# Decode attention of the fox heads: one 128-column query block against one 32-column tile per head pair

## The chip, the cores and the metric

The kernel runs on one core of a Trainium2 chip. The metric is the device time of one execution in microseconds, the median of several runs. TensorE has two clock levels, 1.2 and 2.4 GHz; the profile gives the granted clock of a stretch as a share of the higher one (PEclk). In the profile PE is TensorE's matrix passes, PEld its weight loads, DVE VectorE, ACT ScalarE, POOL GpSimd and SP SyncE, which issues the DMAs.

## What is computed

One layer of a hybrid encoder: a feed-forward block, a token mixer with two groups of attention heads (latent attention, "MLA", and forgetting attention, "fox"), and a second feed-forward block. There are 1,024 prompt frames, and 8 running streams of 16 new frames, each with 512 cached rows. The change touches only the fox heads of the 8 streams. Cut to that:

```python
# per stream: q (16, 8, 64), k and v (512 + 16, 8, 64), cumulative log forgets lq, lk
s = einsum('qhd,khd->hqk', q, k) * 64 ** -0.5
s = s + (lq - lk)                      # per head
s = where(k_pos <= q_pos, s, -inf)
p = softmax(s, axis=-1)
o = einsum('hqk,khd->qhd', p, v)
```

## The kernel before

The program is written in stages, one block of engine programs each: feed-forward 1, input projection, latents, MLA of the prompt, `sample_setup`, `sample_attention` (the 8 streams), fox of the prompt, output projection, feed-forward 2. The feed-forward blocks are some three quarters of the time and are left as they are.

`sample_attention` runs the 8 streams in a loop of two (b = 0 and 1), with the last two written out. The order on each engine is the order of the code; engines meet at semaphores. In one step PE does, for stream n and the one after it:

1. `stream`: transposes of the probabilities of stream n (L1514 cached, L1518 new rows), into PSUM; ACT copies them to `pT` and `pTn`.
2. `transpose_keys`: transposes of the keys of stream n + 1 (L1480), in seven groups over two PSUM banks, which ACT and DVE empty in turn (L1385, L1380). Names: `ckv` and `kr` are the MLA keys, `fk` the fox keys.
3. `score` of stream n + 1 (L1485, L1502): `scores` has 128 partitions, 16 for each of the 8 heads, and a column for each of the 528 keys. The MLA scores come from `qc` and `qr`. The fox scores come from `qf`, the block-diagonal query: its 512 depth rows (8 heads of 64) lie in 4 chunks `c` of 128, and chunk c has the 128 query columns with all but those of heads 2c and 2c + 1 at zero. So 4 matmuls accumulate over c, each 128 rows deep and 128 columns wide, over 512 cached keys (`fkT`) and again over 16 new ones (`knT`); one more matmul (`qa` with `aug_r`) adds the forget sums, and one the mask.
4. The value products of stream n (L1531 over 4 row groups `r` of the cache, L1532 for the new rows): `out_bank[0]` for MLA with `ckv`, then `out_bank[1]`, which is `o_ps`, for fox. The fox product takes all 128 probability columns with all 512 value columns (8 heads of 64), so 128 x 512 results, of which each partition needs its own head's 64.

All these matmuls are f32; the trace shows each of them as two passes with a weight load each, the transposes as one. DVE takes the row maxima (L1428, L1432), then `outputs`: the reciprocal of the sums, the MLA result (L1440), and for fox three steps: `picked` = `o_ps` times a 0/1 head mask, 128 x 512 (L1444), `folded` = the sum over the 8 heads (L1446), and that times the reciprocal into `o_fox` (L1448). ACT takes the exponents of stream n + 1 (L1396) while PE does step 4. POOL copies the queries of the next stream into `qc`, `qr`, `qf`, `qa` (L1369 to L1372). After the last stream all engines meet, and the stage `back` (L1564 on) turns the results.

```python
for m in range(2):
    pe.wait_ge(pt_ok, n2 + 2)
    ...
    rows, new_rows, w = (ckv[b], cn[b], KVL) if m == 0 else (fv[b], vn[b], FW)
    for r in range(CK):
        pe.matmul(out_bank[m][:, 0:w], pT[m][:, r, :], rows[:, r, :], start=(r == 0), stop=False)
```

Of the kernel before, what the change touches and what calls it, by code (L numbers as in the profile page):

```python
# [8 lines left out]
P = 128  # L9
D = 1024  # L10
KD = D // P
SEQ, DECB, DECT, PAST = 1024, 8, 16, 512
# [464 lines left out]
H = 8  # L477
# [649 lines left out]
KEYS = PAST + NEW  # L1127
BH = DECB * H
# [23 lines left out]
def sample_setup(nc, ident, q_sample, select, rows_in, load_first_keys, s):  # L1152
# [3 lines left out]
    with Tools(nc, "setup") as k:  # L1156
# [12 lines left out]
        with k.block() as block:  # L1169
# [59 lines left out]
            def _(dve):  # L1229
# [6 lines left out]
                for j in range(2):  # L1236
                    for c in range(4):
                        src = flip[64 * j:64 * j + 64, 1, c * P:c * P + P].rearrange("p (b t) -> p b t", t=NEW)
                        last = dve.tensor_scalar(s["qbd"][64 * j:64 * j + 64, c, :, (2 * c + j) * NEW:(2 * c + j + 1) * NEW], src, 64 ** -0.5, None, ALU.mult)
# [36 lines left out]
def sample_attention(nc, ident, ident_bf, mask_bf, head_pick, s, cache_ckv, cache_krope, cache_fk, cache_fv, fox_rows, ckv_out, o_rows, prompt_rows, prompt_loaded, keys_in):  # L1276
# [4 lines left out]
    with Tools(nc, "dec") as k:  # L1281
# [16 lines left out]
        picked = k.sb("picked", [P, H, 64])  # L1298
# [26 lines left out]
        inverse_ok, picked_ok, folded_ok, mla_taken, fox_taken = [k.sem(n) for n in ("inverse_ok", "picked_ok", "folded_ok", "mla_taken", "fox_taken")]  # L1325
        LOADS, STAGES, FLIPS = 3, 4, 7
# [12 lines left out]
        with k.block() as block:  # L1339
# [84 lines left out]
            def _(dve):  # L1424
# [9 lines left out]
                def outputs(i, b):  # L1434
                    n, n2 = i * 2 + b, i * 4 + 2 * b
                    dve.wait_ge(exp_ok, n2 + 2)
                    dve.reciprocal(inverse[:, b, :], total[:, b, :]).then_inc(inverse_ok, 1)
                    dve.wait_ge(inverse_ok, n + 1)
                    dve.wait_ge(pv_ok, n2 + (4 + 1))
                    dve.tensor_scalar(o_mla[:, bass.ds(n, 1), :], out_bank[0][:, 0:KVL].unsqueeze(1), inverse[:, b, 0:1], None, ALU.mult).then_inc(mla_taken, 1)  # L1440

                    dve.wait_ge(pv_ok, n2 + (4 + 2))
                    dve.wait_ge(folded_ok, n + 1)
                    dve.tensor_tensor(picked[:, :, :], o_ps[:, :].rearrange("p (h d) -> p h d", h=H), head_pick.unsqueeze(2).broadcast_to([P, H, 64]), ALU.mult).then_inc(fox_taken, 1)  # L1444
                    dve.wait_ge(fox_taken, n + 2)
                    dve.tensor_reduce(folded[:, :], picked[:, :, :].rearrange("p h d -> p d h"), axis=AX.X, op=ALU.add).then_inc(picked_ok, 1)  # L1446
                    dve.wait_ge(picked_ok, n + 1)
                    dve.tensor_scalar(o_fox[:, bass.ds(n, 1), :], folded[:, :].unsqueeze(1), inverse[:, b, 1:2], None, ALU.mult).then_inc(folded_ok, 1)  # L1448
# [16 lines left out]
            def _(pe):  # L1465
# [4 lines left out]
                for free in (mla_taken, fox_taken, folded_ok):  # L1470
                    pe.sem_inc(free, 1)
# [16 lines left out]
                def score(i2, b, last_stream=None):  # L1488
                    n = i2 * 2 + b
                    new = bass.ds(n * NEW, NEW)  # L1490
                    def copied(groups):

                        for e in range(2):
                            pe.wait_ge(flip_ok[e], i2 * FLIPS + (flip_number(b, groups) + 1 - e) // 2)

                    pe.wait_ge(staged, n * STAGES + STAGES)
                    copied(KC + 1)
                    product(cached_part[0], [(qc[b][:, c, :], ckvT[:, c, :]) for c in range(KC)] + [(qr[b][:, :], krT[:, :])], False)
                    if last_stream is not None:
# [5 lines left out]
                    product(cached_part[1], [(qf[b][:, c, :], fkT[:, c, :]) for c in range(4)] + [(qa[b][:, :], s["aug_r"][:, 0:PAST].rearrange("q (p r) -> q r p", r=CK))], False).then_inc(s_ready, 1)  # L1505

                def stream(i, b, follows):
# [17 lines left out]
                    for m in range(2):  # L1525
                        pe.wait_ge(pt_ok, n2 + 2)
                        if m == 1:
                            pe.wait_ge(fox_taken, n + 1)
                        rows, new_rows, w = (ckv[b], cn[b], KVL) if m == 0 else (fv[b], vn[b], FW)
                        for r in range(CK):  # L1530
                            pe.matmul(out_bank[m][:, 0:w], pT[m][:, r, :], rows[:, r, :], start=(r == 0), stop=False)  # L1531
                        pe.matmul(out_bank[m][:, 0:w], pTn[m][:, :], new_rows[:, :], start=False, stop=True).then_inc(pv_ok, 1)  # L1532
# [183 lines left out]
def layer(nc, x_prompt, x_sample, cache_ckv, cache_krope, cache_fk, cache_fv, cache_logf, g1_pre, g1_post, w1_gu, w1_down,  # L1716
# [11 lines left out]
    with Tools(nc, "all") as k:  # L1728
# [3 lines left out]
        tri, ones, head_pick = k.sb("tri", [P, P]), k.sb("ones", [P, P]), k.sb("head_pick", [P, H])  # L1732
        consts_in = k.sem("consts_in")

        with Tools(nc, "consts") as c:
            wide = c.sb("wide", [P, 2 * P + NEW])
            with c.block() as block:
# [8 lines left out]
                def _(dve):  # L1746
# [3 lines left out]
                    dve.tensor_copy(mask_bf[:, :], wide[:, :])  # L1750

# [34 lines left out]
        with Tools(nc, "mix") as m:  # L1786
            fox_loaded = m.sem("fox_loaded")
            logf, krope = m.sb("logf", [P, TT, H]), m.sb("krope", [P, TT, ROPE])
            with Tools(nc, "lat") as l:
# [15 lines left out]
                    qbd=[P, 4, DECB, P], qcT=[P, KC, DECB, H, NEW], aug_l=[P, DECB, P], knT=[P, 4, P], cnT=[P, KC, P], krnT=[ROPE, P],  # L1805
# [13 lines left out]
            with Tools(nc, "dec_all") as d:  # L1819
# [10 lines left out]
                sample_attention(nc, ident, ident_bf, mask_bf[:, 2 * P:2 * P + NEW], head_pick[:, :], own, cache_ckv, cache_krope, cache_fk, cache_fv, fox_rows, ckv_out, acc, fox_prompt_rows, fox_loaded, keys_in)  # L1830
# [55 lines left out]
```

## Time and profile before

| | |
|---|---|
| median of 3 runs | 2846.46 us (2845.43 to 2851.75) |
| span of the profiled execution, which is all the time that its page gives | 2846.8 us |
| PE busy | 2649.1 us, 93% |
| weight loads / DVE / ACT / POOL busy | 82% / 33% / 23% / 15% |
| mean granted clock of TensorE | 0.958 |
| the 8 streams of `sample_attention` | 1433 to 1639 us |

Busy shares are means over the whole span, and weight loads run beside passes. What the streams cost is read from a timeline of PE between 1433 and 1639 us, where a row gives the start, the time to the end of the last pass in it, engine, line, operation, tiles and shape, how many passes, and in brackets how long PE was idle before it and who ended that. Passes are pipelined, so that the time a row really takes is the distance from its start to the start of the next row.

### The profile page before, as it was taken

What the parts mean: (1) busy time and instruction counts of PE and PEld (TensorE: products, weight loads), DVE (VectorE), ACT (ScalarE), POOL (GpSimd) and SP (SyncE); (2) the same over time, 40 slices, a digit from 0 to 9 for tenths busy, and PEclk for the clock granted to TensorE, in tenths of its full rate; (3) what the DMA queues carried; (4) which work ended last, traced back from release to release, by engine and by line L of the source; (5) the groups of instructions that cost most, each with busy time, mean ns of one, the idle gap of its engine ahead of it and who ended that gap; (6) DMA issues with size and microseconds to landing.
All of it is one profiled execution on the core that took longest, in us unless ns stands there. A gap on an engine that the chain in (4) does not pass through costs nothing. (4 is left out here: it accounts for less than half of the span.)

```text
span 2846.8 us, 35924 instructions
## 1 busy us (share of the span) xinstructions
PE 2649.1 (93%) x14251; PEld 2340.2 (82%) x14251; DVE 938.1 (33%) x1612; ACT 658.4 (23%) x1138; POOL 437.9 (15%) x229
## 2 busy tenths in 40 slices
PE   5999999999996997889889969989899999999997
PEld 5999999999995887768745448867899999999996
DVE  4222222222226222554422254434222222222224
ACT  4111111111124011434222214433311111111112
POOL 1111111111113000000000001022111111111112
PEclk8999999999998998989989979989899999999999
DMA  4111111111014221100133030022211111111103
GB/s 152 45 44 44 44 44 44 44 44 44 15 63 156 78 80 39 38 9 0 54 116 115 31 119 0 0 94 92 81 45 44 44 44 44 36 38 44 44 15 141
DMA packets 134646, 161.61 MB, mean 57 GB/s; under 512 B 9648, under 2 KB 105008, under 8 KB 132528
## 3 DMA queue, kind: packets, MB, share of 16 engines
q1 hardware_dynamic: 134576, 160.66, 17.5%
q8 instruction: 47, 0.77, 0.1%
q14 instruction: 23, 0.19, 0.0%
HBM read 138.04 MB, written 22.60 MB: 56 GB/s over the span
## 5 line engine op out<-in xcount | busy, mean ns | idle before, releaser
L65 PE MATMUL ffn_gate_ps<-all_xT_hi,ffn_gu_hi 128*128 128x384 f32 x1056 | 355.8, 337 | 20.4 <-DVE all_xT_lo L163 12.2
L378 DVE TENSOR_TENSOR ffn_prod<-ffn_up_ps,ffn_silu 128x384 f32<-128x384 f32 x132 | 73.6, 558 | 893.2 <-ACT ffn_silu L346 893.2
L66 PE MATMUL ffn_gate_ps<-all_xT_lo,ffn_gu_hi 128*128 128x384 f32 x1056 | 354.9, 336 | 0.0
L67 PE MATMUL ffn_gate_ps<-all_xT_hi,ffn_gu_lo 128*128 128x384 f32 x1056 | 354.9, 336 | 0.0
L65 PE MATMUL ffn_up_ps<-all_xT_hi,ffn_gu_hi 128*128 128x384 f32 x1056 | 352.9, 334 | 0.0
L67 PE MATMUL ffn_up_ps<-all_xT_hi,ffn_gu_lo 128*128 128x384 f32 x1056 | 352.7, 334 | 0.0
L66 PE MATMUL ffn_up_ps<-all_xT_lo,ffn_gu_hi 128*128 128x384 f32 x1056 | 352.7, 334 | 0.0
L346 ACT ACTIVATE ffn_silu<-ffn_gate_ps 128x384 f32<-128x384 f32 x132 | 64.9, 492 | 1222.3 <-PE ffn_up_ps L67 1222.3
L65 PE MATMUL ffn_down_ps<-ffn_dn_hi,ffn_a_hi 128*128 128x512 f32 x792 | 309.2, 390 | 2.2 <-DVE all_acc L391 2.1
L391 DVE TENSOR_TENSOR all_acc<-ffn_down_ps,all_acc 128x512 f32<-128x512 f32 x360 | 246.0, 690 | 195.1 <-PE ffn_down_ps L67 195.1
L67 PE MATMUL ffn_down_ps<-ffn_dn_hi,ffn_a_lo 128*128 128x512 f32 x792 | 308.6, 390 | 0.0
L66 PE MATMUL ffn_down_ps<-ffn_dn_lo,ffn_a_hi 128*128 128x512 f32 x792 | 308.6, 390 | 0.0
L315 POOL TENSOR_TENSOR ffn_gu_lo<-gu_raw,ffn_gu_hi 128x2048 fp32r<-128x2048 f32 x43 | 197.5, 4613 | 460.1 <-ACT ffn_gu_hi L339 460.1
L319 POOL TENSOR_TENSOR ffn_dn_lo<-ffn_dn_raw,ffn_dn_hi 128x2048 fp32r<-128x2048 f32 x22 | 101.4, 4607 | 855.1 <-ACT ffn_dn_hi L352 855.1
L65 PEld LDWEIGHTS ffn_gate_ps<-all_xT_hi,ffn_gu_hi 128*128 128x128 f32 x1056 | 200.0, 189 | 22.4 <-DVE all_xT_lo L163 12.8
L66 PEld LDWEIGHTS ffn_gate_ps<-all_xT_lo,ffn_gu_hi 128*128 128x128 f32 x1056 | 200.1, 189 | 0.8
L67 PEld LDWEIGHTS ffn_gate_ps<-all_xT_hi,ffn_gu_lo 128*128 128x128 f32 x1056 | 199.8, 189 | 0.0
L65 PEld LDWEIGHTS ffn_up_ps<-all_xT_hi,ffn_gu_hi 128*128 128x128 f32 x1056 | 198.2, 188 | 0.0
L66 PEld LDWEIGHTS ffn_up_ps<-all_xT_lo,ffn_gu_hi 128*128 128x128 f32 x1056 | 198.2, 188 | 0.0
L67 PEld LDWEIGHTS ffn_up_ps<-all_xT_hi,ffn_gu_lo 128*128 128x128 f32 x1056 | 198.2, 188 | 0.0
L65 PEld LDWEIGHTS ffn_down_ps<-ffn_dn_hi,ffn_a_hi 128*128 128x128 f32 x792 | 148.7, 188 | 34.9 <-DVE all_acc L391 4.7
L67 PEld LDWEIGHTS ffn_down_ps<-ffn_dn_hi,ffn_a_lo 128*128 128x128 f32 x792 | 148.7, 188 | 31.1
(348 smaller groups left out, 3947.7 us busy)
## 6 DMA issues: line engine op xcount, KB each, us to landing
gu_raw<-in_w_ffn_gu SPq DMA_DIRECT2D x88, 512.0 KB, 5.1
ffn_dn_raw<-in_w_ffn_down SPq DMA_DIRECT2D x22, 1024.0 KB, 4.9
h<-all_acc SPq DMA_DIRECT2D x18, 512.0 KB, 2.9
dec_high_fk<-in_cache_fox_k SPq DMA_DIRECT2D x8, 1024.0 KB, 5.3
dec_x_fv<-in_cache_fox_v SPq DMA_DIRECT2D x8, 1024.0 KB, 4.7
out_fox<-inp_stage SPq DMA_DIRECT2D x27, 256.0 KB, 2.0
in_raw<-in_w_in SPq DMA_DIRECT2D x6, 1024.0 KB, 7.5
fox_x_rows<-out_fox SPq DMA_DIRECT2D x3, 2048.0 KB, 14.8
```

Source lines behind the costliest of these rows:

```text
L65: pe.matmul(out, w_hi, x_hi, start=first, stop=False)
L66: pe.matmul(out, w_hi, x_lo, start=False, stop=False)
L67: return pe.matmul(out, w_lo, x_hi, start=False, stop=last)
L315: pool.tensor_tensor(gu_lo[j][:, :, :], gu_raw[j][:, :, :], plain(gu_hi[j][:, :, :]), ALU.subtract).then_inc(lo_ok, 1)
L319: pool.tensor_tensor(dn_lo[:, :, :], dn_raw[:, :, :], plain(dn_hi[:, :, :]), ALU.subtract).then_inc(lo_ok, 1)
L346: act.activation(silu[:, u % 2, :], gate_ps[:, u % 2, 0:GN], ACT.Silu).then_inc(silu_ok, 1)
L378: dve.tensor_tensor(prod[:, u % 2, :], up_ps[:, u % 2, 0:GN], silu[:, u % 2, :], ALU.mult).then_inc(prod_ok, 1)
L391: dve.tensor_tensor(dst, down_ps[:, m % DR, :], dst, ALU.add).then_inc(added, 1)
```

## The change

The fox query of a stream becomes 4 tiles of 32 columns (`PAIR`: two heads of 16 frames), one for each chunk c; a tile's result goes to its own 32 partitions, at 0, 32, 64 and 96, and no chunk is added to another. `head_pairs` does so for the cached and for the new keys; forget sums and mask are added over all 128 partitions as before. In the value product each pair's 32 probability columns meet only that pair's 128 value columns: 4 matmuls of 32 x 128 for each row group in the place of one of 128 x 512, and 4 for the new rows. On DVE `pair_pick` (which of the two heads a partition belongs to) times the reciprocal gives two scales for each partition, and two operations of 128 x 64 make `o_fox`. POOL copies a quarter as much for `qf`, and the new keys into `kf_new` besides.

```diff
+PAIR = 2 * NEW
...
-        qf = [k.sb(f"qf{b}", [P, 4, P]) for b in range(2)]
+        qf = [k.sb(f"qf{b}", [P, 4, 2 * NEW]) for b in range(2)]
+        kf_new = [k.sb(f"kf_new{b}", [P, 4, NEW]) for b in range(2)]
...
-        LOADS, STAGES, FLIPS = 3, 4, 7
+        LOADS, STAGES, FLIPS = 3, 5, 7
...
+                        pool.tensor_copy(kf_new[b][:, :, :], s["knT"][:, :, bass.ds(n * NEW, NEW)]).then_inc(staged, 1)
...
+                    dve.tensor_scalar(head_scale[:, b, :], pair_pick, inverse[:, b, 1:2], None, ALU.mult).then_inc(scaled_ok, 1)
+                    dve.wait_ge(scaled_ok, n + 1)
                     dve.wait_ge(pv_ok, n2 + (4 + 2))
-                    dve.wait_ge(folded_ok, n + 1)
-                    dve.tensor_tensor(picked[:, :, :], o_ps[:, :].rearrange("p (h d) -> p h d", h=H), head_pick.unsqueeze(2).broadcast_to([P, H, 64]), ALU.mult).then_inc(fox_taken, 1)
...
-                    dve.tensor_reduce(folded[:, :], picked[:, :, :].rearrange("p h d -> p d h"), axis=AX.X, op=ALU.add).then_inc(picked_ok, 1)
...
-                    dve.tensor_scalar(o_fox[:, bass.ds(n, 1), :], folded[:, :].unsqueeze(1), inverse[:, b, 1:2], None, ALU.mult).then_inc(folded_ok, 1)
+                    dve.tensor_scalar(folded[:, :], o_ps[:, 0:64], head_scale[:, b, 0:1], None, ALU.mult).then_inc(half_ok, 1)
+                    dve.wait_ge(half_ok, n + 1)
+                    dve.scalar_tensor_tensor(o_fox[:, bass.ds(n, 1), :], o_ps[:, 64:P].unsqueeze(1), head_scale[:, b, 1:2], folded[:, :].unsqueeze(1), ALU.mult, ALU.add).then_inc(fox_taken, 1)
...
+                    def head_pairs(out, keys):
+
+                        for c in range(4):
+                            pe.matmul(out[c * PAIR:c * PAIR + PAIR, :], qf[b][:, c, :], keys(c), start=True, stop=False)
+
...
-                    product(new_part[1], [(qf[b][:, c, :], s["knT"][:, c, new]) for c in range(4)] + [(qa[b][:, :], s["aug_r"][:, PAST:KEYS])], True)
+                    head_pairs(new_part[1], lambda c: kf_new[b][:, c, :])
+                    pe.matmul(new_part[1], qa[b][:, :], s["aug_r"][:, PAST:KEYS], start=False, stop=False)
...
+                    head_pairs(cached_part[1], lambda c: fkT[:, c, :])
...
+                    pe.wait_ge(fox_taken, n + 1)
+                    for r in range(CK):
+                        for c in range(4):
+                            rows = slice(c * PAIR, c * PAIR + PAIR)
+                            pe.matmul(o_ps[rows, 0:P], pT[1][:, r, rows], fv[b][:, r, c * P:c * P + P], start=(r == 0), stop=False)
+                    for c in range(4):
+                        rows = slice(c * PAIR, c * PAIR + PAIR)
+                        last = pe.matmul(o_ps[rows, 0:P], pTn[1][:, rows], vn[b][:, c * P:c * P + P], start=False, stop=True)
+                    last.then_inc(pv_ok, 1)
```

On PE, from the fox scores over the cached keys to the value products of one step, before (a row ends in the partitions and columns of the result, and in how many such matmuls follow each other):

```order
L1485 MATMUL dec_scores<-dec_fkT,dec_qf 128x512 x4
L1485 MATMUL dec_scores<-dec_x_aug_r,dec_qa 128x512
L1524 REGISTER_ALU
L1531 MATMUL dec_pT_ps<-dec_ckv,dec_pT 128x256 x4
L1532 MATMUL dec_pT_ps<-dec_cn,dec_pTn 128x256
L1531 MATMUL dec_o_ps<-dec_x_fv_4734,dec_pT 128x512 x4
L1532 MATMUL dec_o_ps<-dec_vn,dec_pTn 128x512
```

and changed:

```order
L1501 MATMUL dec_scores<-dec_fkT,dec_qf 32x512 x4
L1514 MATMUL dec_scores<-dec_x_aug_r,dec_qa 128x512
L1533 REGISTER_ALU
L1536 MATMUL dec_pT_ps<-dec_ckv,dec_pT 128x256 x4
L1537 MATMUL dec_pT_ps<-dec_cn,dec_pTn 128x256
L1542 MATMUL dec_o_ps<-dec_x_fv_4735,dec_pT 32x128 x16
L1545 MATMUL dec_o_ps<-dec_vn,dec_pTn 32x128 x4
```

Nothing changes place: the four score matmuls keep their 512 columns and become 32 partitions each, and five fox value matmuls of 512 columns become twenty of 128.

On DVE, the outputs of one step, before:

```order
L1437 RECIPROCAL dec_inverse<-dec_total 128x2
L1440 TENSOR_SCALAR dec_o_mla<-dec_pT_ps,dec_inverse 128x256
L1444 TENSOR_TENSOR dec_picked<-dec_o_ps,all_head_pick 128x512
L1446 TENSOR_REDUCE dec_folded<-dec_picked 128x64
L1448 TENSOR_SCALAR dec_o_fox<-dec_folded,dec_inverse 128x64
```

and changed:

```order
L1440 RECIPROCAL dec_inverse<-dec_total 128x2
L1443 TENSOR_SCALAR dec_o_mla<-dec_pT_ps,dec_inverse 128x256
L1445 TENSOR_SCALAR dec_head_scale<-all_pair_pick,dec_inverse 128x2
L1448 TENSOR_SCALAR dec_folded<-dec_o_ps,dec_head_scale 128x64
L1450 SCALAR_TENSOR_TENSOR dec_o_fox<-dec_o_ps,dec_head_scale,dec_folded 128x64
```

The scale stands ahead of the wait for the fox product; behind that wait two small operations follow in the place of three, two of which read 512 columns.

## Rows read from the trace of the kernel before

**Rows 1.** Page, its head and part 1: busy us (share) and instructions of each engine.

```profile
span 2846.8 us, 35924 instructions
...
PE 2649.1 (93%) x14251; PEld 2340.2 (82%) x14251; DVE 938.1 (33%) x1612; ACT 658.4 (23%) x1138; POOL 437.9 (15%) x229
```

**Rows 2.** Windows, two steps: length, busy us (instructions) of PE, PEld, DVE, ACT, POOL, clock.

```profile
1493.80:1517.80 24.00, 22.16 (x93) 12.25 (x92) 6.89 (x12) 5.68 (x12) 1.42 (x4) 1.00 0.33 114
1517.80:1544.30 26.50, 25.53 (x93) 13.69 (x92) 6.13 (x11) 6.17 (x13) 1.42 (x4) 0.87 0.30 103
```

**Rows 3.** Timeline of PE, one step.

```profile
1496.24 3.70 PE L1531 MATMUL dec_o_ps<-dec_x_fv,dec_pT 128*128 128x512 f32 x8
1499.87 1.12 PE L1532 MATMUL dec_o_ps<-dec_vn,dec_pTn 16*128 16x512 f32 x2
1500.92 1.09 PE L1514 MATMUL dec_pT_ps<-all_ident,dec_p_sb 128*128 128x128 f32 x8
...
1502.07 1.04 PE L1480 MATMUL dec_flip<-all_ident,dec_high_ckv_in 128*128 128x128 f32 x8
1504.26 0.61 PE L1480 MATMUL dec_flip<-all_ident,dec_high_kr 128*32 128x128 f32 x4 [1.15 <-DVE dec_ckvT L1380]
1504.71 0.60 PE L1480 MATMUL dec_flip<-all_ident,dec_high_fk 128*128 128x128 f32 x4
...
1510.44 1.07 PE L1485 MATMUL dec_scores<-dec_x_knT,dec_qf 128*128 x8
1511.36 0.38 PE L1485 MATMUL dec_scores<-dec_x_aug_r,dec_qa 128*128 128x16 f32 x2
...
1512.45 3.70 PE L1485 MATMUL dec_scores<-dec_fkT,dec_qf 128*128 128x512 f32 x8
1515.99 1.96 PE L1485 MATMUL dec_scores<-dec_x_aug_r,dec_qa 128*128 128x512 f32 x2
1517.77 1.91 PE L1531 MATMUL dec_pT_ps<-dec_ckv,dec_pT 128*128 128x256 f32 x8
```

**Rows 4.** Timeline of PE: the same score passes in five other steps.

```profile
1442.99 5.34 PE L1485 MATMUL dec_scores<-dec_fkT,dec_qf 128*128 128x512 f32 x8
...
1463.69 5.23 PE L1485 MATMUL dec_scores<-dec_fkT,dec_qf 128*128 128x512 f32 x8
...
1536.11 6.56 PE L1485 MATMUL dec_scores<-dec_fkT,dec_qf 128*128 128x512 f32 x8
...
1563.31 6.62 PE L1485 MATMUL dec_scores<-dec_fkT,dec_qf 128*128 128x512 f32 x8
...
1589.46 5.40 PE L1485 MATMUL dec_scores<-dec_fkT,dec_qf 128*128 128x512 f32 x8
```

**Rows 5.** Timeline of DVE in the step of rows 3: the fox outputs.

```profile
1501.03 0.69 DVE L1444 TENSOR_TENSOR dec_picked<-dec_o_ps,all_head_pick 128x512 f32<-128x512 f32 x1 [4.01 <-PE dec_o_ps L1532]
1501.76 1.07 DVE L1446 TENSOR_REDUCE dec_folded<-dec_picked 128x64 f32<-128x512 f32 x1
1502.97 0.25 DVE L1448 TENSOR_SCALAR dec_o_fox<-dec_folded,dec_inverse 128x64 f32 x1 [0.15 <-DVE dec_folded L1446]
1503.52 0.69 DVE L1380 COPY dec_ckvT<-dec_flip 128x512 f32<-128x512 f32 x1 [0.29 <-issue]
```

**Rows 6.** Timeline of ACT in that step: the second of the two exponents.

```profile
1495.43 0.69 ACT L1396 ACTIVATE dec_p_sb<-dec_scores,dec_nmax 128x528 f32<-128x528 f32 x1
```

**Rows 7.** Timeline of all engines at the end of the last stream.

```profile
1636.95 0.69 DVE L1444 TENSOR_TENSOR dec_picked<-dec_o_ps,all_head_pick 128x512 f32<-128x512 f32 x1 [4.12 <-PE dec_o_ps L1532]
...
1638.72 0.25 DVE L1448 TENSOR_SCALAR dec_o_fox<-dec_folded,dec_inverse 128x64 f32<-128x64 f32 x1
...
1639.30 0.41 PE L1564 MATMUL dec_flip<-all_ident,dec_o_mla 128*128 128x128 f32 x2 [2.39 <-PEq L1339]
```

**Rows 8.** Line L1480, the narrow weight loads: ns min/median/max, first and last start, form.

```profile
L1480 PEld LDWEIGHTS dec_flip<-all_ident,dec_high_kr x32: 93/97/150, 1434.5 to 1606.8; 128*32 128x32 f32 x32
```

More of the change, by code:

```diff
@@ L1238, in _ @@
                         src = flip[64 * j:64 * j + 64, 1, c * P:c * P + P].rearrange("p (b t) -> p b t", t=NEW)
-                        last = dve.tensor_scalar(s["qbd"][64 * j:64 * j + 64, c, :, (2 * c + j) * NEW:(2 * c + j + 1) * NEW], src, 64 ** -0.5, None, ALU.mult)
+                        last = dve.tensor_scalar(s["qbd"][64 * j:64 * j + 64, c, :, j * NEW:(j + 1) * NEW], src, 64 ** -0.5, None, ALU.mult)
                 last.then_inc(moved, 1)
@@ L1273, in _, with sample_attention @@
                 dve.tensor_tensor(grid, grid, s["l_new"][BH:P, :].unsqueeze(1).broadcast_to([BH, BH, NEW]), ALU.mult)
[L1276 removed]
+def sample_attention(nc, ident, ident_bf, mask_bf, pair_pick, s, cache_ckv, cache_krope, cache_fk, cache_fv, fox_rows, ckv_out, o_rows, prompt_rows, prompt_loaded, keys_in):
     with Tools(nc, "dec") as k:
@@ L1469, in _ @@
                 pe.sem_inc(pv_ok, 4)
-                for free in (mla_taken, fox_taken, folded_ok):
+                for free in (mla_taken, fox_taken):
                     pe.sem_inc(free, 1)
@@ L1504, in score @@
                     copied(FLIPS)
-                    product(cached_part[1], [(qf[b][:, c, :], fkT[:, c, :]) for c in range(4)] + [(qa[b][:, :], s["aug_r"][:, 0:PAST].rearrange("q (p r) -> q r p", r=CK))], False).then_inc(s_ready, 1)
+                    head_pairs(cached_part[1], lambda c: fkT[:, c, :])
+                    pe.matmul(cached_part[1], qa[b][:, :], s["aug_r"][:, 0:PAST].rearrange("q (p r) -> q r p", r=CK), start=False, stop=True).then_inc(s_ready, 1)
                 def stream(i, b, follows):
@@ L1524, in stream @@
                     pe.wait_ge(kept, i * 2 + (b + 3))
[L1525 to L1532, printed above, removed]
+                    pe.wait_ge(pt_ok, n2 + 2)
+                    for r in range(CK):
+                        pe.matmul(out_bank[0][:, 0:KVL], pT[0][:, r, :], ckv[b][:, r, :], start=(r == 0), stop=False)
+                    pe.matmul(out_bank[0][:, 0:KVL], pTn[0][:, :], cn[b][:, :], start=False, stop=True).then_inc(pv_ok, 1)
+                    pe.wait_ge(fox_taken, n + 1)
+                    for r in range(CK):
+                        for c in range(4):
[5 more added lines that the diff above has]
+                    last.then_inc(pv_ok, 1)
                 transpose_keys(0, 0)
@@ L1731, in layer @@
         mask_bf = k.sb("mask_bf", [P, 2 * P + NEW], BF16)
-        tri, ones, head_pick = k.sb("tri", [P, P]), k.sb("ones", [P, P]), k.sb("head_pick", [P, H])
+        tri, ones, head_pick, pair_pick = k.sb("tri", [P, P]), k.sb("ones", [P, P]), k.sb("head_pick", [P, H]), k.sb("pair_pick", [P, 2])
         consts_in = k.sem("consts_in")
@@ L1750, in _ @@
                     dve.tensor_copy(mask_bf[:, :], wide[:, :])
+                    dve.tensor_reduce(pair_pick[:, :], head_pick[:, :].rearrange("p (c j) -> p j c", j=2), axis=AX.X, op=ALU.add)
         acc = k.sb("acc", [P, TT, D])
@@ L1804, in layer @@
                 (Region(nc, "dec_x", xT_at, (PT * D + TT * H * QW) * 4), dict(
-                    qbd=[P, 4, DECB, P], qcT=[P, KC, DECB, H, NEW], aug_l=[P, DECB, P], knT=[P, 4, P], cnT=[P, KC, P], krnT=[ROPE, P],
+                    qbd=[P, 4, DECB, 2 * NEW], qcT=[P, KC, DECB, H, NEW], aug_l=[P, DECB, P], knT=[P, 4, P], cnT=[P, KC, P], krnT=[ROPE, P],
                     qrT=[ROPE, DECB, H, NEW], aug_r=[P, KEYS], l_new=[P, NEW], fv0=[P, CK, FW], fv1=[P, CK, FW])))
@@ L1829, in layer @@
                 sample_setup(nc, ident, q_sample, select, setup_in, load_first_keys, own)
-                sample_attention(nc, ident, ident_bf, mask_bf[:, 2 * P:2 * P + NEW], head_pick[:, :], own, cache_ckv, cache_krope, cache_fk, cache_fv, fox_rows, ckv_out, acc, fox_prompt_rows, fox_loaded, keys_in)
+                sample_attention(nc, ident, ident_bf, mask_bf[:, 2 * P:2 * P + NEW], pair_pick[:, :], own, cache_ckv, cache_krope, cache_fk, cache_fv, fox_rows, ckv_out, acc, fox_prompt_rows, fox_loaded, keys_in)
             fox_prompt(nc, ident, ident_bf, mask_bf[:, P:2 * P], tri[:, :], ones[:, :], logf, fox_prompt_rows, fox_loaded, acc,
```

6 lines of the change are left out of this document (2 added, 4 removed).

## The prediction

> **What bounds the kernel now.** I read the page first: PE is busy for 2649.1 of 2846.8 us [rows 1], so the question is what a PE instruction costs in the stage that is changed. Then the windows of that stage, cut at the steps of the stream loop: in 24.00 us PE is busy for 22.16, and DVE, ACT and POOL for 6.89, 5.68 and 1.42 [rows 2]. PE bounds each step. Its weight loads (12.25 us) run beside its passes: the two add up to more than the window. The timeline of PE then gives the prices as distances from start to start [rows 3]: the fox scores over the cached keys take 1515.99 - 1512.45 = 3.54 us for 8 passes (0.4425 each), those over the new keys 1511.36 - 1510.44 = 0.92 (0.115 each), and the whole fox value product 1500.92 - 1496.24 = 4.68. So 9.14 us of a 24 us step are what the change rewrites. In five of the eight steps the cached scores take longer [rows 4]; the window of the third of these has a mean granted clock of 0.87 against 1.00 [rows 2], so a part of it ran at 1.2 GHz. Against the 3.70 of [rows 3] the five cost 1.64 + 1.53 + 2.86 + 2.92 + 1.70 = 10.65 us. Off PE, DVE's fox outputs run from 1501.03 to 1503.22, and its next copy starts at 1503.52 [rows 5]; PE waits 1.15 us for that copy [rows 3]. ACT's exponents end at 1496.12 [rows 6], 4.8 us before PE asks for them at 1500.92.
>
> **The change, part by part.** The profiled execution spans 2846.8 us; the median of the runs is 2846.46. I sum differences and take them from the median.
>
> *Fox scores.* The number of passes and their columns stay: 4 matmuls, two passes each. A pass over 512 columns takes its time whether 128 or 32 query columns are loaded, so a gain needs passes of different tiles to run side by side. No row shows two tiles at once, so the price is bounded: above by passes one after the other (3.54 and 0.92 us, no gain), below by all four tiles at once (two passes: 0.885 and 0.23 us). I take a value between. In the program's order the two passes of a tile follow each other, and the second must wait for the first, since both stream through the same 32 columns of the array. If passes start in order, what can overlap is the second pass of one tile and the first of the next: 4 matmuls take 5 pass times and not 8 or 2. That is 5 x 0.4425 = 2.21 us (-1.33) and 5 x 0.115 = 0.575 (-0.345).
>
> *Fox value product.* It becomes 20 matmuls, 40 passes, of 128 columns with 32-column weights. A pass of just this shape is in the trace, the turn of the rotary keys (128 rows, 32 columns loaded, 128 streamed): 4 in 1504.71 - 1504.26 = 0.45 us, 0.1125 each [rows 3]. One after the other that is 4.50 us, all four tiles at once 1.13, and with the overlap of neighbours 21 x 0.1125 = 2.36. The new rows are only 16 deep: their two passes cost 1.05 us now against 2 x 3.63/8 = 0.91 for full ones [rows 3], so a group of such passes adds 0.14, which I keep. 2.50 in the place of 4.68: -2.18.
>
> *Going in and out of tiles.* The narrow turns stand among full passes and lose nothing (0.1125 against 0.115 for the score passes of the new keys); the 16-deep pair loses 0.14. The three tiled groups are 128 deep and 32 wide like the narrow turns, so I take 0 for two of them; at 0.14 it would be 0.28 us more in each of 8 steps, 2.2 us in all.
>
> Together -3.855 us a step, and 8 steps: **-30.8**. The exponents still hide: after the scores 2.4 us of MLA products remain ahead of the fox product (1493.80, the window's start, to 1496.24 [rows 2, 3]), and ACT is done 2.3 us after the scores.
>
> *DVE.* Behind the fox product 0.69 + 1.07 + 0.15 + 0.25 us [rows 5] become two operations of 128 x 64 with a wait between, 0.25 + 0.15 + 0.25. DVE is free 1.5 us earlier. In steps where DVE empties the first bank of keys (three show this wait; [rows 3] has the first) its copy can then start when the first four turns are done, near 1502.6 and not at 1503.52; what is late next is PE's own turns. I count 0.85 us three times: **-2.5**. After the last stream PE waits for DVE to end [rows 7]: 2.02 us from 1636.95 become 0.65: **-1.35**.
>
> *The rest at nothing.* POOL copies a quarter of `qf` and adds `kf_new`; it works 1.42 us in a step of 24 [rows 2]. The fill of `qbd` gets smaller. `pair_pick` is one small DVE operation at the program's start: +0.25 at most, by the smallest row of [rows 5]; I count it. The arrays behind `pair_pick` move by 32 bytes; no row prices that. The clock I leave as it is; the 10.65 us of [rows 4] could vanish, or recur in other steps at up to 2.92 each (8 x 2.92 - 10.65 = +12.7).
>
> Sum: -30.8 - 2.5 - 1.35 + 0.25 = -34.4, so 2846.46 - 34.4 = **2812**.
>
> **The rivals.**
>
> *A. All four tiles run at once.* The second pass of a tile does not hold up the next tile. Scores 0.885 and 0.23, values 10 x 0.1125 + 0.14 = 1.27: -6.76 a step, -54.1 in 8, with the other terms -57.7: **2789**. For it: the tiles share neither columns nor result partitions. Against: each tile has two passes in a row. The Trainium skill ("TensorEngine Tiling (Array Packing)", Theoretical Speedup) gives up to 4x for a dimension of 32; no run here shows it so far, and by it the time would be that of this rival.
>
> *B. Nothing overlaps, loads stay hidden.* The tiles then are the same passes in other shapes: values 4.64 for 4.68, scores unchanged. Only DVE's terms remain: -0.3 - 3.6 = -3.9, **2842.5** (2845 with the price of going in and out). For it: every pair of passes in the trace is strictly one behind the other. Under 0.2% (5.7 us), which is about what a measurement of this kernel tells from no change.
>
> *C. Nothing overlaps and the loads show: slower.* A pass now uses one tile's columns, and the load for the next tile waits until it is over. A narrow load takes 0.097 us [rows 8], and there are 40 in the value product for 10. 48 loads (40 and the 8 of the cached scores) x 0.097 = 4.66 us a step, 37.3 in 8, less 3.9: **2880**. It decides from 3.9/(8 x 48) = 10 ns of each load in the open. Against: today's loads are hidden, though all of them use the full depth of 128 rows like the passes that hide them [rows 2]. The Trainium skill ("TensorE: Matmul & The Clock Gate", The mechanism) has loads overlap running passes only where their row groups differ, with a background buffer as another way; here row groups never differ. By that rule alone the time would be this rival's; the windows speak for the buffer.
>
> *D. The clock.* The tiled passes run at 1.2 GHz throughout. By [rows 4] against [rows 3] a group then takes 1.82 times as long (6.46 for 3.54). One after the other that is +2.9 and +3.65 us a step: 52.4 - 10.65 - 3.6 = +38, **2885**. With neighbours overlapped the groups come to 4.02, 1.05 and 4.44 us: +0.36 a step, -11 in all, 2835, inside my range.
>
> **How the numbers follow.** Overlap of neighbours 0.42, A 0.22, B 0.19, C 0.12, D 0.05. The range goes from A's 2789, less a little for the clock, to B's upper 2845, plus a little: 2786 to 2848; it leaves out C and D, 0.17. The likeliest case alone spans 2801 (the clock's loss gone) to 2835. Faster by over 0.2% is the first two cases, 0.64; within it B, 0.19; slower 0.17.
>
> **What would show it.** Right: the cached fox scores near 2.2 us from start to start at full clock, the value product near 2.5, weight loads and passes of different tiles at the same time in the timeline, the wait for DVE's copy at the turn of the rotary keys gone or under 0.4 us, and steps of some 20 us. A: 0.9 and 1.3 us. B: 3.5 and 4.6. C: 8 us or more for the value product, and PE idle between passes. D: windows with a clock of 0.5 over these groups. I would be wrong as well if a step's end came to hang on ACT's exponents: PE would then wait at the transposes of the probabilities (L1523).

## The result and the profile after

The changed kernel takes 2785.15 us, the median of 4 runs (2781.05 to 2789.74), against 2849.11 us for the kernel before, the median of 4 runs taken with it (2845.43 to 2852.90). The ratio is 0.9776, 95% interval 0.9761 to 0.9791: 64 us faster. A second measurement, beside other runs of the kernel before, gave 2785.26 us and 0.9774 (0.9748 to 0.9799). The forecast was 2812 with a range from 2786 to 2848; the sign is right, the gain is nearly twice the forecast one (64 us for 34), and the time lies just under the low end. It is rival A's mechanism, and a loss of clock that went besides.

The profiled execution spans 2788.0 us (2789.74 with what lies around it). The page's head and part 1, beside [rows 1]:

```profile
span 2788.0 us, 36382 instructions
...
PE 2596.2 (93%) x14491; PEld 2321.9 (83%) x14491; DVE 924.8 (33%) x1613; ACT 659.9 (24%) x1138; POOL 434.2 (16%) x237
```

There are 240 more passes, and PE is busy 52.9 us less. The share of 93% is what it was: it tells nothing of the change. The steps of the stream loop do, in the windows view, beside [rows 2] (length, busy us and instructions of PE, PEld, DVE, ACT, POOL, then clock, DMA share, GB/s):

```profile
1482.60:1499.30 16.70, 15.67 (x122) 9.39 (x121) 5.58 (x12) 5.70 (x12) 1.28 (x5) 1.00 0.46 165
1499.30:1516.10 16.80, 15.82 (x123) 9.37 (x122) 4.91 (x11) 6.19 (x13) 1.28 (x5) 1.00 0.45 163
1532.80:1550.40 17.60, 16.62 (x123) 9.96 (x122) 4.91 (x11) 6.19 (x13) 1.28 (x5) 0.95 0.18 62
```

A step that took 24.00 us takes 16.70, and PE still bounds it. The groups of such a step, in the timeline of PE, answer to [rows 3]; the last four rows are of two other steps and of the end:

```profile
1485.10 1.08 PE L1542 MATMUL dec_o_ps<-dec_x_fv,dec_pT 128*32 128x128 f32 x32
1486.11 0.42 PE L1545 MATMUL dec_o_ps<-dec_vn,dec_pTn 16*32 16x128 f32 x8
1486.46 1.09 PE L1523 MATMUL dec_pT_ps<-all_ident,dec_p_sb 128*128 128x128 f32 x8
...
1488.99 0.61 PE L1482 MATMUL dec_flip<-all_ident,dec_high_kr 128*32 128x128 f32 x4 [0.35 <-DVE dec_ckvT L1383]
...
1495.17 0.26 PE L1501 MATMUL dec_scores<-dec_kf_new,dec_qf 128*32 128x16 f32 x8
1495.36 0.40 PE L1509 MATMUL dec_scores<-dec_x_aug_r,dec_qa 128*128 128x16 f32 x2
...
1496.47 1.07 PE L1501 MATMUL dec_scores<-dec_fkT,dec_qf 128*32 128x512 f32 x8
1497.47 2.04 PE L1514 MATMUL dec_scores<-dec_x_aug_r,dec_qa 128*128 128x512 f32 x2
1499.33 1.91 PE L1536 MATMUL dec_pT_ps<-dec_ckv,dec_pT 128*128 128x256 f32 x8
...
1532.79 2.73 PE L1536 MATMUL dec_pT_ps<-dec_ckv,dec_pT 128*128 128x256 f32 x8
1535.44 0.69 PE L1537 MATMUL dec_pT_ps<-dec_cn,dec_pTn 16*128 16x256 f32 x2
...
1579.10 0.41 PE L1578 MATMUL dec_flip<-all_ident,dec_o_mla 128*128 128x128 f32 x2 [1.07 <-PEq L1341]
```

From start to start: cached fox scores 1497.47 - 1496.47 = 1.00 us (3.54 before), new keys 0.19 (0.92), fox value product 1486.46 - 1485.10 = 1.36 (4.68). The cached scores take 0.99 or 1.00 us in all eight steps; the long ones of [rows 4] are gone. What is left of them shows behind: in two of eight steps the MLA product takes 2.65 and 2.53 us for 1.84, and the window of the first has a clock of 0.95.

To compare kernels I measure the **stage** in the timeline of PE, from its first key turn to the first turn of the stage behind: 1432.72 to 1639.30, 206.58 us, before, and 1436.69 to 1579.10, 142.41 us, after. That is -64.2, what the medians say; the spans differ by 58.8 only, because this execution came to the stage 4.0 us later and took 1.4 us more behind it, in code that is the same but for `pair_pick` and a smaller fill of `qbd` (a second profile of the changed kernel came to the stage at 1433.95). The 64.2 us, each term from these timelines, all eight steps:

| term | forecast, us | measured, us | how |
|---|---|---|---|
| cached fox scores at full clock | -10.6 | -20.3 | 8 x (1.00 - 3.54) |
| new-key scores | -2.8 | -5.8 | 8 x (0.19 - 0.92) |
| fox value product | -17.4 | -26.6 | 8 x (1.36 - 4.68) |
| clock: long cached scores gone | 0 | -10.6 | five groups, 28.33 us, less 5 x 3.54 |
| clock: two slow MLA products | 0 | +1.5 | 2.65 + 2.53 - 2 x 1.84 |
| waits for DVE's copy | -2.5 | -2.0 | 1.15 + 1.13 + 0.80 against 3 x 0.35 |
| wait at the end | -1.35 | -1.3 | 2.39 to 1.07 |
| forget sums behind the tiles | 0 | +0.7 | 8 x (1.87 - 1.78) |
| sum | -34.4 (with `pair_pick`'s +0.25) | -64.4 | |

### The profile page after: what moved, and what is told of

It is laid out like the page before. It is cut to its first block and busy times, and to the rows that moved or that the text cites. A ratio compares the mean times of both kernels' runs of the same rounds, so it can differ in the third digit from the quotient of the medians.

```text
span 2788.0 us, 36382 instructions
## 1 busy us (share of the span) xinstructions
PE 2596.2 (93%) x14491; PEld 2321.9 (83%) x14491; DVE 924.8 (33%) x1613; ACT 659.9 (24%) x1138; POOL 434.2 (16%) x237
```

## The experiments

Three things were open. What lets the tiles run at once (the tiles' being different, or only their narrow weights; any order, or this one), where the lost clock went, and whether the forget sums, now the costliest fox part of a score, can be cheaper. Of the tiles, theory 1 in the expectations has them run at once, theory 2 has passes start in order so that only neighbours overlap; of the clock, theory 1 ties its falls to the short passes of the new keys, theory 2 does not. Each kernel has the changed kernel as its base where nothing else is said; one execution was profiled of each, beside the kernel before on the same chip.

**The same passes, all on one tile.** Every fox value matmul writes partitions 0 to 31, so that three of four pairs' outputs are left out.

```diff
+                dve.memset(o_ps[:, :], 0.0)
...
-                            pe.matmul(o_ps[rows, 0:P], pT[1][:, r, rows], fv[b][:, r, c * P:c * P + P], start=(r == 0), stop=False)
+                            pe.matmul(o_ps[0:PAIR, c * P:c * P + P], pT[1][:, r, rows], fv[b][:, r, c * P:c * P + P], start=(r == 0), stop=False)
...
```

(c is the outer loop, with each pair's new rows behind its four row groups.)

> The changed kernel with all fox value matmuls (same 32-column weights, same 128 columns) on the first tile, the four pairs in four column ranges of its 32 partitions, pair after pair with its new rows; the fox outputs of three of four pairs are left out of the result. If the gain is tiles side by side: 40 passes one behind the other at 0.1125 us and up to 0.14 for each of the four turns to 16-deep passes, 4.5 to 5.1 us for the value product in the place of 1.36, the stage 25 to 30 us longer than 142.4. If narrower weights or fewer columns by themselves make the gain: under 3 us.

Timeline of PE, the first pair of one step and the start of the second:

```profile
1483.39 1.06 PE L1543 MATMUL dec_o_ps<-dec_x_fv,dec_pT 128*32 128x128 f32 x8
1484.39 0.40 PE L1544 MATMUL dec_o_ps<-dec_vn,dec_pTn 16*32 16x128 f32 x2
1484.72 1.06 PE L1543 MATMUL dec_o_ps<-dec_x_fv,dec_pT 128*32 128x128 f32 x8
```

A pair takes 1.33 us (8 passes 1.00, two 16-deep ones 0.33), the product 5.29 for 1.36, the stage 172.01 us, the run 2814.62. So narrow weights alone give nothing, and less than nothing beside the 4.68 of the one wide product: the gain is four tiles side by side. The product came out 0.2 us over what was expected: 8 passes in a row take 1.00 us and not 8 x 0.1125 = 0.90.

**The loops exchanged: a pair's passes in a row.**

```diff
-                    for r in range(CK):
-                        for c in range(4):
+                    for c in range(4):
+                        for r in range(CK):
```

> The changed kernel with the 16 fox value matmuls over the cache in another order: all four row groups of a pair first, then the next pair, so that the passes that stand next to each other in the program are on one tile; the 4 for the new rows stay behind them. Theory 1, each tile runs its passes on its own and waits only for its own earlier passes: the value product stays near 1.36 us from start to start, the stage (first key turn to first turn of the stage behind) near 142.4 us. Theory 2, passes start in the program's order, and the four tiles ran together only because neighbours were on different tiles: of 8 passes on a tile only the last overlaps the next tile's first, 29 pass times of 0.107 us and 0.35 for the new rows, 3.5 us; the stage is 17 us longer, near 160.

The timeline of PE, the fox value product of one step:

```profile
1481.84 2.46 PE L1542 MATMUL dec_o_ps<-dec_x_fv,dec_pT 128*32 128x128 f32 x32
1484.23 0.42 PE L1545 MATMUL dec_o_ps<-dec_vn,dec_pTn 16*32 16x128 f32 x8
```

The 32 passes take 2.39 us, the product 2.74, the stage 152.5, the run 2794.86. That is neither of the two times expected: the order matters, but not as much as in-order starts with only neighbours overlapping would have it. The starts of the single passes say why. The trace does not name a pass's tile; the tiles are told apart as four trains of starts, each some 0.11 us from start to start. The first tile's eight start at 1481.835 and then every 0.11 us to 1482.624; the second tile's first starts at 1482.302, 5 ns behind the first tile's fifth (1482.297), the third tile's at 1482.769, the fourth's at 1483.236. A tile begins when the one ahead of it has three passes left. So I formed another theory, 1a in the expectations below: passes are handed out in program order, each tile has a short queue of its own, one running and three waiting, and a fifth pass in a row holds up everything behind it.

**Two and three row groups of a pair in a row** test that: four passes in a row just fit, six do not.

```diff
-                    for r in range(CK):
+                    for part in ((0, 1), (2, 3)):
                         for c in range(4):
...
+                            for r in part:
```

(with `((0, 1, 2), (3,))` for three)

> The changed kernel with the fox value matmuls over the cache in another order: two row groups of a pair (four passes on one tile), then of the next pair, then the other two row groups of each. Theory 1a, passes are handed out in program order and each tile has a short queue of its own: in the run with four row groups in a row the second tile began with the fifth pass of the first, so one pass runs and three wait; four passes in a row fit, and all tiles still run together: 1.0 to 1.1 us for the 32 passes, 1.4 with the new rows. Theory 2, neighbours on different tiles overlap and nothing else: 25 pass times of 0.1075 us, 2.7, with the new rows 3.0.

> The same with three row groups of a pair in a row (six passes on one tile), then the fourth row group of each pair. Theory 1a: the last of six passes finds room when the third starts, so each tile begins 0.22 us after the one ahead of it; the last one starts at 0.66, runs six passes and then the two of the fourth row group, 8 x 0.11 more: 1.5 us for the 32 passes, 1.9 with the new rows. Theory 2: 2.7 and 3.0 as in the run with two.

Timeline of PE, one step; two in a row, then three:

```profile
1484.58 1.12 PE L1543 MATMUL dec_o_ps<-dec_x_fv,dec_pT 128*32 128x128 f32 x32
1485.63 0.42 PE L1546 MATMUL dec_o_ps<-dec_vn,dec_pTn 16*32 16x128 f32 x8
```

```profile
1485.23 1.81 PE L1543 MATMUL dec_o_ps<-dec_x_fv,dec_pT 128*32 128x128 f32 x32
1486.97 0.42 PE L1546 MATMUL dec_o_ps<-dec_vn,dec_pTn 16*32 16x128 f32 x8
```

The 32 passes take 1.05 us with four passes in a row on a tile (1.01 with two in the changed kernel), 1.74 with six and 2.39 with eight; the runs took 2788.88 and 2792.55 us. Four cost almost nothing, as the queue has it: all four tiles begin within 0.04 us (1484.580 to 1484.620). One waiting room for four passes, shared by all tiles, would fit the exchanged loops as well, but it would have kept the third tile back to the first tile's third pass, which starts at 1484.822 here (an estimate, from these starts). With six a tile should begin when the one ahead has started its third pass, and so it does: the second tile at 1502.907, 6 ns behind the first tile's third pass, the others at 1503.155 and 1503.403. The 1.74 is 0.2 over the 1.5 expected: the tiles begin 0.25 us apart and not 0.22, so that the last one begins 0.09 us later, and its eight passes in a row take 0.99 us, as on the one tile above, and not 8 x 0.11 = 0.88.

**One part of the change at a time, for the clock.** First the kernel before with only the scores over the new keys tiled:

```diff
-                    product(new_part[1], [(qf[b][:, c, :], s["knT"][:, c, new]) for c in range(4)] + [(qa[b][:, :], s["aug_r"][:, PAST:KEYS])], True)
+                    for c in range(4):
+                        pe.matmul(new_part[1][2 * c * NEW:2 * c * NEW + 2 * NEW, :], qf[b][:, c, 2 * c * NEW:2 * c * NEW + 2 * NEW], kf_new[b][:, c, :], start=True, stop=False)
...
```

> The kernel before with nothing but the scores over the 16 new keys in tiles (0.92 us to 0.19 a step). Theory 1 on the clock, the stretch of very short passes ahead of the cached fox scores brings the fall to 1.2 GHz in that group, and a shorter stretch brings it less often: at most 2 of the 8 cached groups take over 4.5 us, the stage goes from 206.6 to 190 to 194 us. Theory 2, the long cached group itself meets the fall: about five of the eight groups still take over 4.5 us, the stage near 201 us.

Timeline of PE, the cached fox scores, which are as before, of four steps in a row:

```profile
1485.04 3.70 PE L1487 MATMUL dec_scores<-dec_fkT,dec_qf 128*128 128x512 f32 x8
...
1508.31 5.40 PE L1487 MATMUL dec_scores<-dec_fkT,dec_qf 128*128 128x512 f32 x8
...
1532.53 5.40 PE L1487 MATMUL dec_scores<-dec_fkT,dec_qf 128*128 128x512 f32 x8
...
1557.49 3.70 PE L1487 MATMUL dec_scores<-dec_fkT,dec_qf 128*128 128x512 f32 x8
```

Four of the eight are long, all by 1.7 us, and none by 2.9 as two are in [rows 4]; the stage takes 195.32 us, the run 2839.35 (2845.27 before beside it). This stands between the two expectations and settles neither: four is near theory 2's five, and the stage is near theory 1's 194. The other way round, the changed kernel with the new keys as before (`qf` block-diagonal again):

```diff
-                    head_pairs(new_part[1], lambda c: kf_new[b][:, c, :])
-                    pe.matmul(new_part[1], qa[b][:, :], s["aug_r"][:, PAST:KEYS], start=False, stop=False)
+                    product(new_part[1], [(qf[b][:, c, :], s["knT"][:, c, new]) for c in range(4)] + [(qa[b][:, :], s["aug_r"][:, PAST:KEYS])], True)
...
```

> The changed kernel but for the scores over the new keys, which are those of the kernel before (0.92 us a step, and the 128-wide query): cached fox scores near 1.0 us, value product near 1.36. Theory 1 on the clock (short passes bring the fall): the fall comes in about five of eight steps and reaches into the forget sums and the MLA products behind, stage 151 to 157 us. Theory 2 (the long cached group met it): falls as rare as in the changed kernel, two steps, stage near 148 us (142.4 and 8 x 0.73).

Timeline of PE, cached fox scores and MLA products where the clock fell, and one step where it did not:

```profile
1444.66 1.89 PE L1506 MATMUL dec_scores<-dec_fkT,dec_qf 128*32 128x512 f32 x8
...
1466.20 3.09 PE L1529 MATMUL dec_pT_ps<-dec_ckv,dec_pT 128*128 128x256 f32 x8
...
1500.16 1.07 PE L1506 MATMUL dec_scores<-dec_fkT,dec_qf 128*32 128x512 f32 x8
...
1503.02 1.91 PE L1529 MATMUL dec_pT_ps<-dec_ckv,dec_pT 128*128 128x256 f32 x8
```

The stage takes 151.62 us, the run 2792.68; the cached groups take 1.82, 1.86, 1.61, 0.99, 1.00, 1.00, 0.99 and 1.76, and two MLA products 3.02 and 2.82. The slow stretches are back in five of eight steps, as theory 1 has it. They cost less than before, 5.3 us and not 10.6 over these two groups. Two more, each one part alone on the kernel before. The value product, with DVE's outputs as in the change:

```diff
+                    for r in range(CK):
+                        for c in range(4):
+                            rows = slice(c * PAIR, c * PAIR + PAIR)
+                            pe.matmul(o_ps[rows, 0:P], pT[1][:, r, rows], fv[b][:, r, c * P:c * P + P], start=(r == 0), stop=False)
...
```

> The kernel before with nothing but the fox value product in tiles, and the DVE outputs that go with it; scores as before. Tiles on their own queues: 4.68 to 1.36 us a step, 26.6 in 8; 1.3 at the end of the last stream and some 2 in DVE's waits: 206.6 to 176.5 us for the stage, with the falls of the clock in the cached scores as before (10.65 us); 10 less if those go with the value product, which neither theory on the clock says.

And the cached scores:

```diff
+                    for c in range(4):
+                        pe.matmul(cached_part[1][2 * c * NEW:2 * c * NEW + 2 * NEW, :], qf[b][:, c, 2 * c * NEW:2 * c * NEW + 2 * NEW], fkT[:, c, :], start=True, stop=False)
...
```

> The kernel before with nothing but the fox scores over the cached keys in tiles: 3.54 to 1.0 us a step at full clock, 20.3 in 8. Theory 1 on the clock (the stretch of short passes brings the fall): falls in about five steps again, in the short group and what stands behind it, some 5 us in the place of 10.65, the stage near 181. Theory 2 (the long cached group met it): two falls or fewer, near 177.

Timelines of PE, the cached fox scores of three steps, with the value product alone tiled; then two of the kernel with the cached scores alone tiled, with two MLA products:

```profile
1485.59 3.70 PE L1485 MATMUL dec_scores<-dec_fkT,dec_qf 128*128 128x512 f32 x8
...
1505.84 6.59 PE L1485 MATMUL dec_scores<-dec_fkT,dec_qf 128*128 128x512 f32 x8
...
1528.66 5.40 PE L1485 MATMUL dec_scores<-dec_fkT,dec_qf 128*128 128x512 f32 x8
```

```profile
1511.51 1.07 PE L1506 MATMUL dec_scores<-dec_fkT,dec_qf 128*32 128x512 f32 x8
...
1575.65 1.94 PE L1506 MATMUL dec_scores<-dec_fkT,dec_qf 128*32 128x512 f32 x8
...
1579.48 2.97 PE L1533 MATMUL dec_pT_ps<-dec_ckv,dec_pT 128*128 128x256 f32 x8
...
1612.27 3.63 PE L1533 MATMUL dec_pT_ps<-dec_ckv,dec_pT 128*128 128x256 f32 x8 [1.08 <-ACT dec_pT L1385]
```

The value product alone: stage 178.45 us (176.5 expected), run 2821.22, and its 1.36 us as in the whole change; the falls cost 12.6 us in its cached scores. The cached scores alone: 185.47 (181 or 177 expected) and 2833.61, where the cached groups take 12.4 us and not 8 x 1.00, and four MLA products 4.1 us more than in other steps. Three of these, 2.4 us, stand behind a short group; the fourth, at 1612.27, is the last stream's, has no scores ahead of it and comes behind a wait of 1.08 us. So a fall is not undone by tiling: what ran at 1.2 GHz in the 3.54 us of the old group runs, in part, in the MLA products behind the short one.

Steps of the eight in which the cached scores are slow, or the MLA product behind them: with the new keys untiled 5 (before), 6 (value product alone), 6 (cached scores alone), 5 (all but the new keys); with them tiled 4 (new keys alone), 2 (the change), 1 (the change, second profile), 1 (loops exchanged), 1 and 1 (two and three in a row), 0 (one tile). Ahead of each of these falls stands a stretch of passes of 16 columns, from the new-key scores to the cached ones. It lasts 1512.45 - 1510.44 = 2.01 us before ([rows 3]) and 1496.47 - 1495.17 = 1.30 after. In the changed kernel the falls come later still: in the windows view, the clock of the one step is 1.00 through this stretch and the tiled scores behind it, and then 0.54 over the forget sums; in the other step it is 0.50 over them.

```profile
1526.00:1530.92 4.92, 4.92 (x31) 2.05 (x29) 1.51 (x3) 0.50 (x1) 0.00 (x0) 1.00 0.67 234
1530.92:1532.79 1.87, 1.87 (x7) 0.69 (x4) 0.01 (x1) 0.00 (x0) 0.00 (x0) 0.54 0.64 261
...
1565.20:1567.17 1.97, 1.97 (x7) 0.81 (x4) 0.01 (x1) 0.00 (x0) 0.00 (x0) 0.50 0.00 0
```

The forget sums take 1.87 and 1.97 us there, and 1.87 at full clock: the fall costs them next to nothing. In the tiled kernels they lie where the long cached scores lay, which is a part of why a fall is cheaper there.

Not every fall in the stage follows 16-column passes. The one at 1612.27 above does not, and in ten of the twelve profiles the clock falls around the first key turns of the second step, behind a wait of PE of 1.6 us (0.76 to 0.83 us for the turn of the rotary keys, which takes 0.45 otherwise). Shortening the stretch goes with fewer falls in both pairs that differ in it alone (5 and 4; 5 and 2 or 1). But one execution was profiled of each kernel, and two profiles of the same kernel differ by one step as well (2 and 1): that the short passes bring the falls is not shown, and that shortening them does not remove the falls by itself, the four of the first pair show.

**The forget sums read in their order.** In both kernels the two passes that add the cached forget sums take 0.9 us each (1.78 us before, [rows 3], and 1.87 after), twice a fox pass of the same 512 columns (0.4425, [rows 3]). They stream `aug_r` with a step of 16 bytes from element to element. Here it is laid down once, at the setup, in the order in which it is read:

```diff
-                dve.tensor_scalar(s["aug_r"][0:BH, :], cum[:, :], -1.0, None, ALU.mult)
+                dve.tensor_scalar(s["aug_r"][0:BH, 0:PAST].rearrange("q (r p) -> q r p", r=CK), cum[:, 0:PAST].rearrange("q (p r) -> q r p", r=CK), -1.0, None, ALU.mult)
+                dve.tensor_scalar(s["aug_r"][0:BH, PAST:KEYS], cum[:, PAST:KEYS], -1.0, None, ALU.mult)
...
-                    pe.matmul(cached_part[1], qa[b][:, :], s["aug_r"][:, 0:PAST].rearrange("q (p r) -> q r p", r=CK), start=False, stop=True).then_inc(s_ready, 1)
+                    pe.matmul(cached_part[1], qa[b][:, :], s["aug_r"][:, 0:PAST], start=False, stop=True).then_inc(s_ready, 1)
```

> The changed kernel with the cached part of the forget sums laid down once, in the setup, in the order in which the score matmul streams them (one more small DVE operation there), so that its 512 columns are read side by side and not one in four. If the strided read is what makes these two passes 0.93 us each where other passes of 512 columns take 0.44: 1.86 us become 0.9 to 1.0 a step, the stage 7.5 us shorter, near 135, and the whole some 0.26% faster than the changed kernel; the exponents stay hidden behind MLA and fox products (3.8 us for 2.3). If the passes are slow for another reason (the step from tiles to full width, the weights): nothing moves, 142.

Timeline of PE, one step, and then the windows of two steps:

```profile
1487.12 1.06 PE L1502 MATMUL dec_scores<-dec_fkT,dec_qf 128*32 128x512 f32 x8
1488.12 1.13 PE L1515 MATMUL dec_scores<-dec_x_aug_r,dec_qa 128*128 128x512 f32 x2
1489.08 1.89 PE L1537 MATMUL dec_pT_ps<-dec_ckv,dec_pT 128*128 128x256 f32 x8
```

```profile
1473.30:1489.08 15.78, 14.75 (x123) 9.35 (x121) 5.58 (x12) 5.68 (x12) 1.28 (x5) 1.00 0.51 178
1489.08:1504.91 15.83, 14.86 (x123) 9.33 (x121) 4.90 (x11) 6.17 (x13) 1.28 (x5) 1.00 0.48 174
```

The sums take 0.96 us for 1.87, eight times, so the strided read was the reason, and not the step from tiles to full width. No step has a slow group, and the second step's turns are not slow either; the stage takes 132.06 us, 9.5 less than in the changed kernel's second profile below. The sums are 7.3 of this, against 7.5 expected; the rest is mostly falls of the clock that did not come in this execution. The time is 2773.46 us, median of 5 (2773.13 to 2777.89), against 2845.16 for the kernel before (median of 9): ratio 0.9742, interval 0.9717 to 0.9767. It is faster than both kernels, by some 12 us than the changed one, which ran again on the same chip:

> The changed kernel itself, once more, beside the next one on the same chip: tiles on their own queues give a cached fox score group of 1.0 us, 0.19 for the new keys and a value product of 1.36 in every step; the stage is 142 us give or take the clock's falls, of which I expect none to three (up to 1.7 us each), so 140 to 144.

That second profile of the changed kernel has a stage of 141.51 us, the same 1.00, 0.19 and 1.36, and one slow MLA product (2.58).

## Why the prediction was right and wrong

**The step that failed** is "If passes start in order, what can overlap is the second pass of one tile and the first of the next: 4 matmuls take 5 pass times and not 8 or 2." They take two. Narrow windows of the changed kernel's timeline, on the first and on the second half of the cached scores that start at 1496.47:

```profile
1496.47 0.16 PEld L1501 LDWEIGHTS dec_scores<-dec_fkT,dec_qf 128*32 128x32 f32 x8
1496.47 0.64 PE L1501 MATMUL dec_scores<-dec_fkT,dec_qf 128*32 128x512 f32 x4
...
1496.93 0.61 PE L1501 MATMUL dec_scores<-dec_fkT,dec_qf 128*32 128x512 f32 x4
```

Four passes start within 20 ns, the tiles' second passes 0.45 us later, and all eight weight loads lie in the first 0.16 us. A second pass waits for its own tile alone, in that tile's queue, and holds up nobody. The premise that second passes wait was right; that a waiting pass blocks those behind it is true only from the fifth in a row on, as the loops exchanged and the two splits showed. The sentence was written as the point on which the case hung ("If passes start in order"), but no row of one-tile code could decide it, and I took the value between the bounds where the better bound was the truth. Rival A's prices were near: 0.885 against 1.00, 0.23 against 0.19, 1.27 against 1.36 us. In eight steps the three groups gave 20.3 + 5.8 + 26.6 = 52.7 us, where the forecast had 30.8 and rival A 54.1. For the four tiles the Trainium skill ("TensorEngine Tiling (Array Packing)", Theoretical Speedup) gives up to 4x; the traces agree in kind, with 3.54/1.00 = 3.5 and 4.68/1.36 = 3.4.

**The clock**, "I leave as it is", was the other miss, -9.1 us in the table. The prediction had noted that the 10.65 us could vanish, but put that into the range and not into the sum; and it gave them in full to the likeliest case only, while rival A's end of the range, 2786, has 3 us of them. That is why the time fell out of the range although A is in it. Over the cached scores and the MLA products behind them the loss is 10.6 us before, 12.6 with the value product alone tiled, 6.9 with the cached scores alone, 6.8 (4 x 1.7) with the new keys alone, 5.3 with all but the new keys, and 1.5 and 0.7 in the two profiles of the changed kernel. So no one part removes it, and all together nearly do. A part of this is seen: a fall that reaches over the forget sums costs little there. What brings a fall, and why it comes in one step and not in the next, stays open.

**Going in and out of tiles** I priced at nothing, with 2.2 us in all as the other value. The forget sums behind the tiles went from 1.78 to 1.87 (+0.7 us in all), and the cached scores and the 32 value passes take 0.11 us more each than two and eight pass times (1.00 for 0.885, 1.01 for 0.90), which is 1.8 us in eight steps. So the other value was near, if all of this is put down to the tiles; no run takes it apart. The 0.14 for the 16-deep passes held: their group takes 0.35 us, 0.13 over two passes of 0.11.

**DVE** came out as worked out: its two outputs start at 1503.30 and 1503.73 in the step below, where three operations ran before ([rows 5]).

```profile
1502.42 0.22 DVE L1445 TENSOR_SCALAR dec_head_scale<-all_pair_pick,dec_inverse 128x2 f32<-128x2 f32 x1
1503.30 0.28 DVE L1448 TENSOR_SCALAR dec_folded<-dec_o_ps,dec_head_scale 128x64 f32<-128x64 f32 x1 [0.66 <-PE dec_o_ps L1545]
1503.73 0.28 DVE L1450 SCALAR_TENSOR_TENSOR dec_o_fox<-dec_o_ps,dec_head_scale,dec_folded 128x64 f32 x1
```

The wait at the turn of the rotary keys is 0.35 us, under the 0.4 given, and what is late there is PE's own turns, as said; the end lost 1.3 us for 1.35. ACT's exponents stayed hidden: the transposes of the probabilities at 1486.46 show no wait.

**The other rivals.** B (nothing overlaps) and D (1.2 GHz throughout) are refuted by the 1.00 us at full clock. C needs loads in the open: the line view has, for the value product's 32-column loads (count, ns min/median/max, first and last start, form):

```profile
L1542 PEld LDWEIGHTS dec_o_ps<-dec_x_fv,dec_pT x256: 106/110/110, 1468.3 to 1577.3; 128*32 128x32 f32 x128
```

32 of them in a step are 3.5 us, and the 32 passes they serve take 1.01 from start to start: they run beside the passes and beside each other. All use the same four row groups. The Trainium skill ("TensorE: Matmul & The Clock Gate", The mechanism) lets a load overlap running passes only where row groups differ, and names a background weight buffer besides; with row groups that never differ, the loads of different column tiles overlap passes here, so these runs do not agree with that rule by itself. It also has passes start in program order throughout; with the loops exchanged the second tile's first pass starts at 1482.302, ahead of the first tile's sixth at 1482.406, which precedes it in the program, and so these runs do not agree there either.

## What to carry to other kernels

A matmul that uses a quarter of its output (a block-diagonal query, an all-pairs product of which each partition keeps one part) is worth splitting into 32-column tiles, each on its own 32 partitions: here the passes became 3.4 to 3.5 times cheaper, with the loop over the tiles inside. Up to four passes in a row on one tile cost next to nothing more (1.05 us for 1.01), six and eight cost 1.74 and 2.39. Read such a stage by distances from start to start of its groups, not by busy shares, and look at how the streamed operand lies in memory: a step of 16 bytes doubled a pass here (0.89 us for 0.44). Where the trace cannot decide between two bounds, let the case hang on the one missing fact and give both ends their weight, the good one too.

## What was not expected of the hardware

- Each of the four column tiles takes one running and three waiting passes, by the starts with four, six and eight in a row: 32 passes on four tiles cost 1.01, 1.05, 1.74 and 2.39 us with two, four, six and eight in a row on a tile.
- The first passes of four tiles start 7 ns apart, and quartets follow every 0.11 us, the price of one pass.
- A pass that streams 512 f32 columns takes 0.44 us where they lie in a row and 0.89 with a step of 16 bytes (0.48 and 0.93 behind tiles), and the latter hardly more at a granted clock of 0.50 (two passes 1.97 us, 1.87 at full clock).
- Behind a stretch of 16-column passes the granted clock fell in 5 or 6 of 8 steps where it lasted 2.0 us, and in 0 to 4 where it lasted 1.3, in one execution of each kernel; that the stretch is the cause is not shown. The fall costs what runs behind it: 1.5 to 2.9 us in the old cached scores, 0.0 to 0.1 in the forget sums.
